# Splitting three of the MLP's seven down operands where their rows are made: one decoder layer, float32, on one NeuronCore

## The reference, cut to what matters

```python
h = x + rms_norm(m, n_mix_post)
f = jnp.square(jax.nn.relu(rms_norm(h, n_ffn_pre) @ w_up)) @ w_down   # 1024 -> 4096 -> 1024
return h + rms_norm(f, n_ffn_post), new_buf, S_new
```

## Time and profile before

| | |
|---|---|
| median of three runs | 1622.49 us |
| profiled execution, its span | 1625.69 us, 1623.6 us |
| TensorE busy | 1546.5 us, 95% |
| VectorE busy | 944.0 us, 58% |
| GpSimd busy | 709.7 us, 44% |
| ScalarE busy | 510.1 us, 31% |
| mean granted TensorE clock | 0.987 of full speed |
| HBM read, written | 124.82 MB, 43.36 MB |

### The profile page before, as it was taken

The page is one execution under the profiler, slowest core; times in us unless marked ns, Lnnn a source line. Parts: engine busy times, 40 slices in busy tenths (PEclk is TensorE's granted clock), DMA queues, the critical chain, the costliest instruction groups (busy, mean ns, idle before and its releaser), DMA issues.

```text
span 1623.6 us, 27821 instructions
## 1 busy us (share of the span) xinstructions
PE 1546.5 (95%) x10948; PEld 1524.3 (94%) x10948; DVE 944.0 (58%) x1192; ACT 510.1 (31%) x697; POOL 709.7 (44%) x508
## 2 busy tenths in 40 slices
PE   6999999999999999999999999999999999999993
PEld 5999999999999898999999999999999999999892
DVE  6899959754474234201152885555556766675856
ACT  4100101422320225000022666544446242423332
POOL 3444444442244222344446464454445454555554
PEclk9999999999999999999999999999999999999996
DMA  5211121123221231111142023644447633434332
GB/s 174 91 46 47 50 61 46 40 77 101 81 92 45 79 104 59 39 45 45 45 150 79 14 96 129 246 149 145 147 148 281 219 126 118 136 127 152 105 136 105
DMA packets 83527, 169.45 MB, mean 104 GB/s; under 512 B 7392, under 2 KB 19424, under 8 KB 81136
## 3 DMA queue, kind: packets, MB, share of 16 engines
q1 hardware_dynamic: 69504, 144.61, 27.3%
q10 hardware_dynamic: 13936, 23.60, 4.4%
HBM read 124.82 MB, written 43.36 MB: 104 GB/s over the span
## 4 chain that ended last, share of the span: by engine, by line
PE 84%; DVE 10%; issue 2%; ACT 2%; DMA 1%; POOL 0%; DVEq 0%; ACTq 0%; SPq 0%
PE ps L630 44%; PE ps L973 30%; PE ps L889 3%; DVE tx_l L418 3%; DVE fx_l L418 1%; PE ps L902 1%; PE ps L812 1%; PE ps L730 1%; PE ps L729 1%; DVE xn_l L1591 1%; PE ps L733 1%; DVE fac L2002 1%; PE ps L744 1%; DMA x_in<-xT_dram 1%; DVE x_in L1587 1%
## 5 line engine op out<-in xcount | busy, mean ns | idle before, releaser
L540 POOL TENSOR_TENSOR w_h<-raw,zero 128x512 fp32r<-128x512 f32 x130 | 144.7, 1113 | 520.7 <-PE ps L630 399.0
L973 PE MATMUL ps<-tx_h,w_h 128*128 128x258 f32 x960 | 272.9, 284 | 11.0 <-DVE fac L2002 5.3
L973 PE MATMUL ps<-tx_l,w_h 128*128 128x258 f32 x960 | 271.9, 283 | 0.0
L973 PE MATMUL ps<-tx_h,w_l 128*128 128x258 f32 x960 | 271.9, 283 | 0.0
L599 POOL TENSOR_TENSOR w_l<-raw,w_h 128x512 fp32r<-128x512 f32 x120 | 181.0, 1509 | 178.5 <-ACT w_h L1366 178.3
L630 PE MATMUL ps<-xn_h,w_h 128*128 128x344 f32 x1128 | 249.5, 327 | 2.4 <-DVE xn_l L1591 1.4
L630 PE MATMUL ps<-xn_l,w_h 128*128 128x344 f32 x1128 | 242.5, 321 | 0.0
L630 PE MATMUL ps<-xn_h,w_l 128*128 128x344 f32 x1128 | 241.3, 320 | 0.0
L973 PE MATMUL ps<-fx_h,w_h 128*128 128x258 f32 x720 | 204.4, 284 | 6.7 <-DVE fac L2048 3.9
L973 PE MATMUL ps<-fx_h,w_l 128*128 128x258 f32 x720 | 203.3, 282 | 0.0
L973 PE MATMUL ps<-fx_l,w_h 128*128 128x258 f32 x720 | 203.1, 282 | 0.0
(11 more groups left out here) (273 smaller groups left out, 2582.6 us busy)
## 6 DMA issues: line engine op xcount, KB each, us to landing
raw<-wseq_dram SPq DMA_DIRECT2D x264, 256.0 KB, 2.7
hq_g<-hidden_scratch SPq DMA_DIRECT2D x14, 1032.0 KB, 8.1
hidden_scratch<-hq_g SPq DMA_DIRECT2D x8, 1032.0 KB, 5.6
stg_a<-hidden_scratch SPq DMA_DIRECT2D x7, 1032.0 KB, 7.9
stg_b<-hidden_scratch SPq DMA_DIRECT2D x7, 1032.0 KB, 7.7
hidden_scratch<-stg_b SPq DMA_DIRECT2D x6, 1032.0 KB, 5.8
rope<-rope_dram ACTq DMA_DIRECT2D x2, 2064.0 KB, 8.0
h_res<-xT_dram ACTq DMA_DIRECT2D x1, 4128.0 KB, 14.2
```

What stands on the lines that cost most here:

```text
L540: pool.tensor_tensor(hi, raw[:, s, :], zero[:, 0:1].broadcast_to([P, SLOT]), ALU.add).then_inc(w_hi, 1)
L973: out = pe.matmul(ps[:, 2 * n + s, 0:HC], RINGS[q % RING][wa][:, kk * P:(kk + 1) * P], OPS[x][xb][:, QK * kh + kk, at_:at_ + HC], start=(i ...
```

## The change

Of the seven down operands, those of products 2, 3 and 4 (rows 4, 5 and 6 of each unit) are split unit by unit in the up phase. ScalarE copies the three rows to a new buffer `quad_h` (`hidden_hi`, 128x1548), VectorE subtracts that from the rows in place (`hidden_lo`, 128x1548). SyncE stores the high parts to a new DRAM scratch `qscr` and rows 4 to 7 (three of them low parts now) to `uscr` (`store_quads`, 0.77 + 1.03 MB); `store_unit` keeps two transfers. At a group's start SyncE loads high and low part of these three operands, 1.03 MB each, straight into their quadrants of `tx_h` and `tx_l` (`load_quads`, six transfers), each pair when the last product that reads the old quadrant is done; TensorE waits for the landing (`q_ld`). Products 0, 1, 5 and 6 go on as before (`SPLIT`), with one staging place each. The work is placed anew in the programs of VectorE, ScalarE and SyncE. New waits: `hidden_sums` waits until the rows 4 to 7 that it overwrites are stored (`quads_stored` on VectorE), `hidden_hi` until the `quad_h` before is stored. Units 14 and 15 lie in new buffers. Room is made by a smaller scratch area (`SCRATCH` = 1024 bytes in place of 16384).

```diff
+    qscr = nc.dram_tensor("quad_scratch", (GROUPS, 3, P, QK, HT), F32, kind="Internal").ap()
-        at = [16512]
+        at = [SCRATCH + 128]
+        quad_h, _ = place("quad_h", [P, 3, HT], F32R)
...
         def stored(e, u):
-            e.wait_ge(st_u[u % 2], 48 * (u // 2 + 1))
+            e.wait_ge(st_u[u % 2], 32 * (u // 2 + 1))
+        def quads_stored(e, u):
+            e.wait_ge(st_q[u % 2], 32 * (u // 2 + 1))
+        SPLIT = (0, 1, 5, 6)
...
+            def store_quads(u):
+                g, j = divmod(u, QK)
+                sp.wait_ge(u_lo, u + 1)
+                sp.dma_start(qscr[g, :, :, j, :].rearrange("s p n -> p s n"), quad_h[:].bitcast(F32)).then_inc(st_q[u % 2], 16)
                 sp.dma_start(uscr[g, 3:7, :, j, :].rearrange("s p n -> p s n"), hq_rows(u, 4, 8)
-                             ).then_inc(st_u[u % 2], 16)
+                             ).then_inc(st_q[u % 2], 16)
+            def load_quads(g):
+                for u in (QK * g + 2, QK * g + 3):
+                    quads_stored(sp, u)
+                for i in range(2, 5):
+                    x, kh, th = X_OF[i]
+                    sp.wait_ge(pm, step_done(UPV + QK * g - 1, i))
+                    sp.dma_start(tx_h[:, KHALVES[kh], HALVES[th]].bitcast(F32), qscr[g, i - 2]).then_inc(q_ld[i - 2], 16)
+                    sp.dma_start(tx_l[:, KHALVES[kh], HALVES[th]].bitcast(F32), uscr[g, OP_SLOT[i]]
+                                 ).then_inc(q_ld[i - 2], 16)
             store_unit(0)
             for v in range(NV):
+                if v == 0:
+                    store_quads(0)
                 if v == UPV - 1:
                     stored(sp, UNITS - 4)
-                    load_operand(2)
-                    load_operand(3)
+                    quads_stored(sp, UNITS - 4)
+                    load_operand(0, 0)
+                    load_operand(0, 1)
                     stored(sp, UNITS - 3)
-                    load_operand(0)
-                    load_operand(1)
+                    quads_stored(sp, UNITS - 3)
+                    load_operand(0, 2)
+                    load_operand(0, 3)
...
+                if v >= UPV - 1 and p == 3 and v + 1 < NV:
+                    load_quads(g + 1)
-                if d <= 0:
+                if d < 0:
                     store_unit(v + 1)
+                if d < -1:
+                    store_quads(v + 1)
+                if d == 1:
+                    store_unit(UNITS - 1)
+                    store_quads(UNITS - 2)
+                if d == 2:
+                    store_quads(UNITS - 1)
...
                 if v >= UPV and (v - UPV) % 4 == 0:
-                    lo_made(pe, STEPS * ((v - UPV) // 4) + i)
+                    if i in SPLIT:
+                        lo_made(pe, (v - UPV) // 4, SPLIT.index(i))
+                    else:
+                        pe.wait_ge(q_ld[i - 2], 32 * ((v - UPV) // 4 + 1))
...
+            def hidden_hi(u):
+                act.wait_ge(t_u, 4 * u + 4)
+                if u:
+                    quads_stored(act, u - 1)
+                act.activation(quad_h[:], hq_rows(u, 4, 7), ACT.Copy).then_inc(u_hi, 1)
...
                 high(v, 3)
+                if v == 0:
+                    hidden_hi(0)
+                if v == UPV - 1:
+                    staged_hi(0, 0)
                 stat(0)
                 high(v, 4)
+                if v == UPV - 1:
+                    staged_hi(0, 1)
...
                 high(v, 6)
+                if v < UPV - 1:
+                    hidden_hi(u - 1)
                 stat(3)
                 next_high(v, 0)
...
                 dve.wait_ge(sq_u, 2 * u + 2)
+                if 2 <= u < UNITS - 2 or u == DIRECT - 1:
+                    quads_stored(dve, u - 2 if u >= 2 else u - 1)
...
+            def hidden_lo(u):
+                dve.wait_ge(u_hi, u + 1)
+                dve.wait_ge(t_u, 4 * u + 4)
+                rows = hq_rows(u, 4, 7)
+                dve.tensor_tensor(rows.bitcast(F32R), rows, quad_h[:].bitcast(F32), ALU.subtract).then_inc(u_lo, 1)
...
                 last_sum(v)
+                if v == 0:
+                    hidden_lo(0)
                 stat(2)
-                hidden_sums(u - 1)
+                if v == UPV - 1:
+                    staged_lo(0, 0)
+                    staged_lo(0, 1)
+                else:
+                    hidden_sums(u - 1)
...
                 stat(7)
                 if v == UPV - 1:
-                    staged_lo(1)
+                    hidden_sums(u - 1)
+                else:
+                    hidden_lo(u - 1)
```

More of the change, by code:

```diff
@@ L303, in build @@
         st_u = [sem("st_u0"), sem("st_u1")]
+        st_q = [sem("st_q0"), sem("st_q1")]
+        u_hi = sem("u_hi")
+        u_lo = sem("u_lo")
+        q_ld = [sem(f"q_ld{i}") for i in range(3)]
         h_sp = sem("h_sp")
```

157 lines of the change are left out of this document (69 added, 88 removed).

## The result

The changed kernel took 1627.8 us (median of 8 runs, 1626.56 to 1632.06), the kernel before beside it 1623.4: ratio 1.0028, 95% interval 1.0018 to 1.0039. It is slower by 4.4 us where 4.9 less were forecast. The profiled executions differ by 1632.06 - 1625.69 = 6.4 us; in the MLP, from the first matmul of iteration 0 to the last of iteration 29, by 7.0 (637.1 against 630.1 us). Single runs of three experiments, 8625.7 (e1), 6038.61 (e3) and 3014.5 us (e7), stand far apart from all others and are left out of the intervals.

A forecast was written before the change was run, and what follows sets the result against it. TensorE's work plus its gaps was taken as the bound, the gaps coming from VectorE being late at group starts. -13.1 + 0.9 + 3.1 + 4.4 - 0.2 = -4.9 us, median 1617.6 us, range 1611.5 to 1624.5.

The forecast's parts named there:

- Groups 1 to 3: Down phase, group starts: waits for VectorE's late additions vanish, -13.1 us, between -13.1 and -11.5.
- Covered, with 7 us left: Groups 1 to 3: six transfers, 6.2 MB at 386 GB/s, take 16 us of the 23.0 us available.
- the sign that the prediction named for rival 2: Iterations 18, 22 and 26 waiting for the landings would show rival 2 right.
- rival 2: Shared queue at 276 GB/s (decisive under about 310) delays group 0 and groups 1 to 3: +11 us, 1634; chance 0.14.
- Group 0: Iterations 13 to 15: new wait of 8.1 us at product 4 of 13, old waits go; +0.9, between -2 and +4.
- Iterations 0 to 2: Product 6 late behind a store, then behind ScalarE's new copy: +3.1 in iteration 0, +2.2 each in 1 and 2.
- Iteration 4: Up phase: its wait of 0.2 us for a store is lost, -0.2 us.
- Plain iterations: Up phase: new copy (1.5 us) and `hidden_lo` (2.2 us) lie in gaps; over 20.3 us would overturn this.
- The size of `hidden_lo`: VectorE's 128x1548 subtraction in the up phase and group 0: 2.2 us taken, between 1.7 and 3.0.
- the rule that the prediction named: VectorE instructions with two SBUF inputs and GpSimd ones reading SBUF exclude each other; `hidden_lo(0)` ends near 973.4, sum +0.9 us.
- Rival 1: Up phase and group 0 eat the whole gain, every new wait at its upper end: +1.7, 1624; chance 0.22.

The follow-up runs named there:

- e1: Changed kernel with unit 1's sums and copy in iteration 0 moved behind the additions and ScalarE's part of the iteration; 1625.3 us, ratio 1.0005.
- e3: Changed kernel with the 4.1 MB store of h in iteration 3 issued after unit 4's two stores; 1625.09 us, ratio 1.0007.
- e7: Changed kernel with group 0's first two staging loads moved ahead of the stores of unit 13's split rows; 1627.58 us, ratio 1.0015.
- e8: Changed kernel with unit 0's copy and low part moved ahead of iteration 0; 1623.75 us, ratio 0.9992.
- e9: e6_combined with iteration 13's weight loads and first split pair queued ahead of the wait for unit 13's split rows; 1609.68 us, ratio 0.9914.
- e5: Changed kernel with 30 further matmuls, results unused, ahead of product 6 of iteration 0; 1626.24 us, ratio 1.0015.
- e6_combined: Changed kernel with the moves of e8, e3 and e7, and the copy in iterations 1 and 2 behind ScalarE's squares; 1611.17 us, ratio 0.9921.

## Why the prediction was wrong, point by point

**Groups 1 to 3: right, by a thinner cover than was worked out.** -12.15 us for -13.1, inside the bounds. Product 5 of 17, 21 and 25 waits for nothing. The 0.9 us that are left are in iteration 18, and they are a wait for the landing of the last pair, issued at 1353.39 and landed 15.0 us later, at 1368.4 (landing, then TensorE):

```profile
tx_l<-hidden_scratch SPq DMA_DIRECT2D x1, 1032.0 KB, 15.0
```

```profile
1368.44 0.36 PE L1009 MATMUL ps<-tx_h,w_h 128*128 128x258 f32 x1 [0.64 <-issue]
```

The view names no releaser ("issue"); that it was the landing is read from the 0.1 us between the two, as in e7, e8 and e9, where a product 4 began just as close behind its last landing. "Covered, with 7 us left" was wrong in size: from the first issue, at 1345.87, to that landing it took 22.5 us and not 16, since 7.8 MB moved in that time, weights among them, at a mean of 347 GB/s, where 6.2 MB at 386 were counted. In iterations 22 and 26 the last pair landed 1.1 and 2.5 us ahead of product 4. In the other executions with this order it came 0.1 to 2.7 us ahead, and all but e8's (121.57) spent 121.0 us in the six iterations, which is no wait at all. So the sign that the prediction named for rival 2 did show, once and small; the gain of groups 1 to 3 had no more than this to spare.

**Group 0: right in place; in size partly by luck.** +1.2 for +0.9. Product 4 of iteration 13 came 6.2 us late, behind e3 and ScalarE's staged copy. The forecast had 8.1; but the store went out 2.5 us into the iteration in place of 3.1, and the second load landed 12.7 us after it in place of 14.0. The 1.6 us that the clock cost behind the wait, which the forecast did not have, filled most of that gap. Iterations 14 and 15 each kept 1.2 us where 1.5 and 0.4 were forecast. The last pair landed 40.5 us after the iteration's start; the forecast had said 1267.3 against a start of 1227.8, 39.5. For this burst rival 2 is out: between 1250 and 1280 the windows show 365, 399 and 391 GB/s, never under 310.

```profile
1250.00:1260.00 10.00, 6.70 (x56) 6.49 (x55) 1.78 (x3) 2.44 (x2) 0.58 (x1) 0.97 1.03 365
1260.00:1270.00 10.00, 7.18 (x47) 7.21 (x48) 7.48 (x6) 5.10 (x8) 7.32 (x4) 0.69 1.03 399
```

**Iterations 0 to 2: right in mechanism, wrong in price. This is the step that failed.** "Product 6 was due a product after e5's 977.68, at 980.5: **+3.1**" and "+2.2 each" put the cost of a wait at its length. The waits measured 3.8 and 2.1 each; but behind each TensorE ran at 0.50 of the clock, which cost 2.4 and 1.5 us more. The trace of before had a case of it that the sum passed over, product 4 of iteration 14 (timeline, then a window):

```profile
1265.73 0.36 PE L973 MATMUL ps<-tx_h,w_h 128*128 128x258 f32 x1 [2.14 <-DVE fac L2000]
```

```profile
1268.00:1270.00 2.00, 2.00 (x11) 2.00 (x10) 2.00 (x3) 0.00 (x0) 0.00 (x0) 0.50 0.29 111
```

It took 4.46 us. Between the forecast -4.9 and the MLP's +7.0 lie 11.9 us: 3.2 in iteration 0, 3.2 in iterations 1 and 2, 3.85 in iteration 4, 0.95 in groups 1 to 3, 0.3 in group 0 and 0.4 in the rest. The four slow products of iterations 0, 1, 2 and 4 make 7.0 of them; e5 took the one of iteration 0 away and left its wait.

**Iteration 4: missed.** "Iteration 4 loses its wait of 0.2 us for a store" took a store's wait for gone, without a walk of the queue, on which `store_quads` with its wait now stands ahead. This term is the second step that failed. The place where a store was already waited for, behind the largest single transfer of the program, was the place to walk, not to count as a gain. It cost 2.2 us of wait and 1.6 of clock; e3 took all of it away.

**Plain iterations: right.** They took 20.13 to 20.18 us, under the 20.3 that would have overturned the term.

**The size of `hidden_lo`:** 2.85 us in iteration 0, against 2.2 taken and 3.0 as the upper bound. Timeline of GpSimd in the changed kernel at that time, then of VectorE and of GpSimd in iteration 13 of e6_combined:

```profile
969.26 1.73 POOL L632 TENSOR_TENSOR w_l<-raw,w_h 128x512 fp32r<-128x512 f32 x1 [1.10 <-ACT w_h L1402]
```

```profile
1228.29 1.76 DVE L1989 TENSOR_TENSOR hq_g<-hq_g,quad_h 128x1548 fp32r<-128x1548 f32 x1
```

```profile
1228.98 2.24 POOL L634 TENSOR_TENSOR w_l<-sum_y,w_h 128x512 fp32r<-128x512 f32 x1 [1.88 <-ACT w_h L1404]
```

In iteration 0 GpSimd's subtraction had started at 969.26, `hidden_lo` at 969.76, and `hidden_lo` took 2.85. In the other row `hidden_lo` started first, took 1.76, and GpSimd's took 2.24 where another took 1.27. The later of the two pays; the rule that the prediction named from the Trainium skill (SBUF - State Buffer, Who interferes with whom) agrees, and its end near 973.4, 3.1 us after the start, was nearer than the 2.2 us taken. That iteration 0's wait was longer by the same 0.7 us is chance: `hidden_lo` took 0.65 us more than forecast and the store 1.0 more, and sums, e5 and e6a together 1.1 less (3.7 us, from 979.96 to 983.68).

**The rivals.** The time lies above the range. No rival was what happened: it ended on rival 2's side, but neither burst as a whole ran under its 310 GB/s, and the landings in groups 1 to 3 cost only the 0.9 us of iteration 18. Rival 1, every new wait at its upper end, comes nearest (iteration 0 +6.3 for 5, iterations 1 and 2 +7.6 for 6), but its ends too were lengths of waits alone.

## What to carry to other kernels

Where TensorE is busy nearly throughout, cost a new wait of two microseconds or more at its length and 1.4 to 2.6 us more for the clock behind it (34 of 35 such waits here had that price; the next product is counted in), and look in the trace for a product that took longer than its neighbours before calling a wait small. Work that frees a busy engine at one place has to be put somewhere; walk it through every iteration that differs from the plain one (here 0, 1, 2, 4 and 13 to 15 of 30), and past every wait that it puts on a shared queue: four moves of order, none of which changed the work, turned +0.3% into -0.8%. Splitting work sooner (e8) gave 6.0 us over iterations 0 to 2; putting other work off (e1) gave 4.9 and left a wait elsewhere.
